# Stick-breaking attention by differences of neighbouring values

## The reference, cut to what matters

```python
z = einsum('bqhd,bshd->bhqs', qb, k) * HEAD_DIM ** -0.5
before = key_pos[None, :] < q_pos[:, None]
log_keep = where(before, log_sigmoid(-z), 0.0)
log_tail = cumsum(log_keep, axis=3, reverse=True) - log_keep
weight = where(before, exp(log_sigmoid(z) + log_tail), 0.0)
out = einsum('bhqs,bshd->bqhd', weight, v)
```

## Time and profile before

| | us |
|---|---|
| median of 3 runs (1811.06 to 1814.52) | 1811.9 |
| time of the profiled execution | 1813.25 |
| span of the profiled execution, first to last instruction | 1811.5 |
| TensorE busy in the span | 1668.0 (92%) |
| VectorE busy in the span | 1167.7 (64%) |
| projection of layer 1, first matmul with a weight to last copy | 1004.6 to 1148.2 |
| stick-breaking attention, first scores to last values | 1149.4 to 1236.8 |

### The profile page before, as it was taken

How to read it: one execution, slowest core, us unless ns; L and a number is a source line. 1 busy time by engine, 2 the same in 40 slices (tenths; PEclk the granted TensorE clock), 3 DMA queues, 4 the chain that set the end, 5 groups by cost and what they waited for, 6 DMA issues and landing times. The chain is left out here.

```text
span 1811.5 us, 27708 instructions
## 1 busy us (share of the span) xinstructions
PE 1668.0 (92%) x10992; PEld 893.3 (49%) x11121; DVE 1167.7 (64%) x1926; ACT 489.6 (27%) x854; POOL 180.2 (10%) x234
## 2 busy tenths in 40 slices
PE   6999988989979999999997999889989999999995
PEld 5656677855543333333332778654533333333332
DVE  5456877774347677767777533593337777777666
ACT  5243334453211111111112422573311111111112
POOL 2000734411000000000000000352100000000000
PEclk9999999989989999999998999999989999999997
DMA  6541000023779999999995220205679999999992
GB/s 166 157 126 36 7 3 3 4 94 116 306 300 418 425 426 428 424 427 425 427 425 213 94 93 24 93 2 220 270 315 425 426 426 426 426 426 426 426 422 113
DMA packets 101186, 471.45 MB, mean 260 GB/s; under 512 B 28864, under 2 KB 67776, under 8 KB 75456
## 3 DMA queue, kind: packets, MB, share of 16 engines
q1 hardware_dynamic: 98752, 461.25, 63.2%
q0 software_dynamic: 2304, 8.39, 1.2%
HBM read 452.84 MB, written 16.78 MB: 259 GB/s over the span
## 5 line engine op out<-in xcount | busy, mean ns | idle before, releaser
L707 PE MATMUL ps<-w_unit,xT 128*48 128x512 f32 x1024 | 454.6, 597 | 4.3 <-DVE xT L764 4.3
L708 PE MATMUL ps<-w_unit,xT 128*48 128x512 f32 x1024 | 454.7, 597 | 0.0
L809 DVE SCALAR_TENSOR_TENSOR x<-ps,gate_by_expert,x 128x512 f32<-128x512 f32 x512 | 348.4, 744 | 139.2 <-PE ps L759 139.0
L707 PEld LDWEIGHTS ps<-w_unit,xT 128*48 128x48 f32 x1024 | 126.6, 124 | 312.1 <-issue 306.6
L737 PE MATMUL ps<-w_unit,hidT 128*48 128x512 f32 x1024 | 249.3, 607 | 12.1 <-issue 12.1
L832 ACT ACTIVATE y_high_low<-y_cut 48x512 fp32r<-48x512 f32 x128 | 80.4, 628 | 403.8 <-DVE y_cut L780 401.4
L759 PE MATMUL ps<-y_high_low,slots_to_tokens 128*128 128x512 f32 x512 | 160.0, 434 | 13.8 <-DVE y_high_low L784 13.1
L759 PEld LDWEIGHTS ps<-y_high_low,slots_to_tokens 128*128 128x128 f32 x512 | 88.8, 194 | 133.2 <-issue 67.8
L1244 PE MATMUL ps<-hT_high,w_high 128*128 128x512 f32 (+1 forms) x344 | 140.0, 407 | 10.1 <-PE ps L1246 3.7
L1246 PE MATMUL ps<-hT_high,w_low 128*128 128x512 f32 (+1 forms) x344 | 136.2, 396 | 0.0
L1245 PE MATMUL ps<-hT_low,w_high 128*128 128x512 f32 (+1 forms) x344 | 135.8, 395 | 0.0
(11 more groups left out here) (365 smaller groups left out, 2241.9 us busy)
## 6 DMA issues: line engine op xcount, KB each, us to landing
w_unit<-in_moe_w SPq DMA_DIRECT2D x184, 2048.0 KB, 27.6
w_unit<-in_moe_w SPq DMA_DIRECT2D x16, 1024.0 KB, 32.3
x_rows<-sorted_rows SPq DMA_DIRECT2D x64, 192.0 KB, 26.2
w_unit<-in_od_w_qkv SPq DMA_DIRECT2D x12, 1024.0 KB, 5.4
w_raw<-in_ev_w_in SPq DMA_DIRECT2D x10, 1024.0 KB, 6.5
sorted_rows<-bias SPq DMA_DIRECT2D x32, 192.0 KB, 5.6
w_unit<-in_ev_w_out SPq DMA_DIRECT2D x2, 2048.0 KB, 11.9
w_unit<-in_od_w_out SPq DMA_DIRECT2D x2, 2048.0 KB, 10.4
```

Source lines behind the costliest of these rows:

```text
L707: nc.tensor.matmul(ps_1[0:MB, :], xT[b][:, k, :], w1[:, k, :], start=k == 0, stop=k == KD - 1)
L708: last = nc.tensor.matmul(ps_3[UP:UP + MB, :], xT[b][:, k, :], w3[:, k, :], start=k == 0, stop=k == KD - 1)
L809: nc.vector.scalar_tensor_tensor(out=xs, in0=ps_c[i % 4][:, :], scalar=gate(t), in1=xs, op0=ALU.mult, op1=ALU.add).then_inc(added, 1)
```

## The change

The sum over keys is taken by parts. Since beta = 1 - keep, the weight of key s is tail(s+1) - tail(s), and the output is the sum over s of tail(s) * (v(s-1) - v(s)), plus v of the last key. The kernel turns the tails themselves and multiplies them with the differences `dv`. In the last block of keys of a unit the last row is v(s-1) alone (`dv_last`), which puts the missing term back. beta, its mask and the product L1462 go; the tail tiles become four.

The differences are made in the projection. The column groups are permuted to v, q, k (`odd_columns`), so v is group 0 to 3. When all banks of v are emptied, SyncE copies v one key (one partition) down into `xn` by seven transfers inside SBUF: four of 127 partitions with 4 KB each and three of one row. They stand ahead of the weight load of group 7. GpSimd then waits for all seven, subtracts four tiles of 128x1024 and copies 127 rows of each difference back.

```diff
+def odd_columns(g):
+    lo = (g * GC + 2 * D) % (3 * D)
+    return slice(lo, lo + GC)
...
 class LoadedAhead:
-            sp.dma_start(self.raw[g], self.w[:, :, g * GC:(g + 1) * GC]).then_inc(self.raw_in[g], 16)
+            sp.dma_start(self.raw[g], self.w[:, :, odd_columns(g)]).then_inc(self.raw_in[g], 16)
...
 def odd_project(...):
-    is_v = lambda g: g >= 2 * D // GC
+    shifted, edge, differed, copied = c.sem("v_shifted"), c.sem("v_edge"), c.sem("v_differed"), c.sem("v_copied")
+    VG, QG = D // GC, 2 * D // GC
+    is_v = lambda g: g < VG
...
+    def shift(sp):
+        for t in range(TT):
+            sp.dma_start(xn[1:P, t, :], v[0:P - 1, t, :]).then_inc(shifted, 16)
+            if t:
+                sp.dma_start(xn[0:1, t, :], v[P - 1:P, t - 1, :]).then_inc(shifted, 16)
...
         @block.sync
         def _(sp):
             for g in range(w.RAW, NG):
-                w.load(sp, g, [(0, w_dram.rearrange("(p k) n -> p k n", k=KD)[:, :, g * GC:(g + 1) * GC])])
+                if g == VG + w.RAW:
+                    for b, (_, emptied) in enumerate(sems):
+                        sp.wait_ge(emptied, VG * TT // 8)
+                    shift(sp)
+                w.load(sp, g, [(0, w_dram.rearrange("(p k) n -> p k n", k=KD)[:, :, odd_columns(g)])])
+        @block.gpsimd
+        def _(pool):
+            pool.wait_ge(shifted, 16 * (2 * TT - 1))
+            nc.gpsimd.memset(xn[0:1, 0, :], 0.0).then_inc(edge, 1)
+            pool.wait_ge(edge, 1)
+            for t in range(TT):
+                nc.gpsimd.tensor_tensor(v[:, t, :], xn[:, t, :], v[:, t, :], ALU.subtract).then_inc(differed, 1)
+                pool.wait_ge(differed, t + 1)
+                nc.gpsimd.tensor_copy(xn[0:P - 1, t, :], v[0:P - 1, t, :]).then_inc(copied, 1)
+            pool.wait_ge(copied, TT)
...
 def stick_breaking(...):
-    beta = [c.sb(f"beta{i}", [P, 2, T], ctx=ctx) for i in range(DEEP)]
-    tail = [c.sb(f"tail{i}", [P, 2, T + 1], ctx=ctx) for i in range(2)]
+    tail = [c.sb(f"tail{i}", [P, 2, T], ctx=ctx) for i in range(DEEP)]
...
-                    pe.wait_ge(beta_done, 2 * (u - 2) + 2)
+                    pe.wait_ge(keep_done, u - 1)
...
-                pe.wait_ge(weighted, u + 1)
+                pe.wait_ge(scanned, 2 * u + 2)
...
-                                                   beta[u % DEEP][:, a, b * P:(b + 1) * P], c.ident[:, :])
+                                                   tail[u % DEEP][:, a, b * P:(b + 1) * P], c.ident[:, :])
...
-                                                v[:, b, h * HD:(h + 1) * HD], wT[u % 2][:, a, b * P:(b + 1) * P],
+                                                (dv_last if b == t else dv)[:, b, h * HD:(h + 1) * HD], wT[u % 2][:, a, b * P:(b + 1) * P],
...
-                    nc.scalar.activation(beta[i % DEEP][:, :, 0:L], ps_z[i % 2][:, :, 0:L],
-                                         ACT.Sigmoid).then_inc(beta_done, 1)
...
-                nc.vector.tensor_tensor(beta[i % DEEP][:, :, 0:L], beta[i % DEEP][:, :, 0:L],
-                                        tail[i % 2][:, :, T - L + 1:T + 1], ALU.mult).then_inc(weighted, 1)
```

More of the change, by code:

```diff
@@ L1264, in dest @@
         if is_v(g):
-            lo = g * GC - 2 * D
-            return v[:, s, lo:lo + GC]
-        f = FG * g + s
+            return v[:, s, g * GC:(g + 1) * GC]
+        f = FG * (g - VG) + s
         return qT[:, f, :] if f < KD else kT[:, f - KD, :]
@@ L1279, in empty_and_split @@
                 b = banks[n % 8]
-                b.empty(copy(dest(g, s), b.read(eng)[:, 0:width(g)], HD ** -0.5 if g < D // GC else 1.0))
+                b.empty(copy(dest(g, s), b.read(eng)[:, 0:width(g)], HD ** -0.5 if VG <= g < QG else 1.0))
             if n + 1 < len(outs) and outs[n + 1][0] != g and g + 2 < NG:
@@ L1327, in stick_breaking @@
 @stage
-def stick_breaking(nc, c, ctx, ps, qT, kT, v, yT, w_out, wts):
+def stick_breaking(nc, c, ctx, ps, qT, kT, dv, dv_last, yT, w_out, wts):
     PAIRS = C_HEADS // 2
@@ L1334, in stick_breaking @@
     keep = [c.sb(f"keep{i}", [P, 2, T], ctx=ctx) for i in range(DEEP)]
-    beta = [c.sb(f"beta{i}", [P, 2, T], ctx=ctx) for i in range(DEEP)]
-    tail = [c.sb(f"tail{i}", [P, 2, T + 1], ctx=ctx) for i in range(2)]
+    tail = [c.sb(f"tail{i}", [P, 2, T], ctx=ctx) for i in range(DEEP)]
     wT = [c.sb(f"wT{i}", [P, 2, T], ctx=ctx) for i in range(2)]
     zero = c.sb("zero", [P, T], ctx=ctx)
-    z_done, beta_done = c.sem("z_done"), c.sem("beta_done")
-    keep_masked, beta_masked = c.sem("keep_masked"), c.sem("beta_masked")
-    scanned, weighted = c.sem("scanned"), c.sem("weighted")
+    z_done, keep_done, keep_masked, scanned = c.sem("z_done"), c.sem("keep_done"), c.sem("keep_masked"), c.sem("scanned")
     turned, wT_out, pv_done, y_out, ready = (c.sem("turned"), c.sem("wT_out"), c.sem("pv_done"),
@@ L1417, in _ @@
                         act.wait_ge(scanned, 2 * (i - DEEP + 1))
-                        act.wait_ge(turned, i - DEEP + 1)
                     nc.scalar.activation(keep[i % DEEP][:, :, 0:L], ps_z[i % 2][:, :, 0:L], ACT.Sigmoid,
-                                         scale=-1.0).then_inc(beta_done, 1)
-                    nc.scalar.activation(beta[i % DEEP][:, :, 0:L], ps_z[i % 2][:, :, 0:L],
-                                         ACT.Sigmoid).then_inc(beta_done, 1)
+                                         scale=-1.0).then_inc(keep_done, 1)
                 u = i - LAG_T
@@ L1437, in _ @@
                 lo, hi = t * P, (t + 1) * P
[L1439 to L1443, removed]
+                pool.wait_ge(keep_done, i + 1)
+                part = keep[i % DEEP][:, :, lo:hi]
+                nc.gpsimd.affine_select(out=part, in_=part, compare_op=ALU.is_gt, fill=1.0, base=0,
+                                        pattern=[[0, 2], [-1, P]], channel_multiplier=1).then_inc(keep_masked, 1)
         @block.vector
@@ L1447, in _ @@
             nc.vector.memset(zero[:, :], 0.0).then_inc(ready, 1)
-            for i in range(2):
-                nc.vector.memset(tail[i][:, :, T:T + 1], 1.0).then_inc(ready, 1)
-            dve.wait_ge(ready, 3)
+            dve.wait_ge(ready, 1)
             for i, (t, f) in enumerate(units):
@@ L1453, in _ @@
                 dve.wait_ge(keep_masked, i + 1)
-                if i >= 2:
-                    dve.wait_ge(weighted, i - 1)
+                if i >= DEEP:
+                    dve.wait_ge(turned, i - DEEP + 1)
                 for a in range(2):
-                    nc.vector.tensor_tensor_scan(tail[i % 2][:, a, T - L:T][:, ::-1],
+                    nc.vector.tensor_tensor_scan(tail[i % DEEP][:, a, 0:L][:, ::-1],
                                                  keep[i % DEEP][:, a, 0:L][:, ::-1], zero[:, 0:L], 1.0,
                                                  ALU.mult, ALU.add).then_inc(scanned, 1)
-                dve.wait_ge(beta_masked, i + 1)
-                dve.wait_ge(scanned, 2 * i + 2)
-                nc.vector.tensor_tensor(beta[i % DEEP][:, :, 0:L], beta[i % DEEP][:, :, 0:L],
-                                        tail[i % 2][:, :, T - L + 1:T + 1], ALU.mult).then_inc(weighted, 1)
 def odd_mixer(nc, c, ps, x, gain, w_qkv, w_out, wts, slots, guests, ahead, held):
@@ L1472, in odd_mixer @@
         v = c.sb("v", [P, TT, D], ctx=inner)
+        xn = c.sb("xn", [P, TT, D], ctx=inner)
         with ExitStack() as proj:
-            xn = c.sb("xn", [P, TT, D], ctx=proj)
             odd_project(nc, c, proj, ps, x, xn, gain, w_qkv, qT, kT, v, ahead)
@@ L1477, in odd_mixer @@
         wts.add_units(guests, GUEST)
-        stick_breaking(nc, c, inner, ps, qT, kT, v, yT, w_out, wts)
+        stick_breaking(nc, c, inner, ps, qT, kT, v, xn, yT, w_out, wts)
     wts.add_units(slots, range(GUEST[0]))
```

## The result

The changed kernel takes 1860.47 us (median of 4 runs, 1857.82 to 1861.76), beside it the kernel before 1811.48 us; the ratio is 1.0275, 95% interval 1.0258 to 1.0291. It is slower by 49 us. Forecast were 1855 us and one transfer engine as the cause.

A forecast was written before the change was run, and what follows sets the result against it. VectorE was taken to bound the attention and TensorE the projection. The terms +2.4 + 0.3 + 52.5 + 2.5 - 14.5 = +43.2 us on the median 1811.9 gave 1855 us, range 1838 to 1902.

The forecast's parts named there:

- attention: Attention stage: without VectorE's product TensorE sets the pace, so the last filler starts earlier, -14.5 us.
- v first: Projection start: narrower v groups do less work while slices of x arrive, +2.4 us.
- last copy wider: Projection end: the last copy is twice as wide, +0.3 us.
- load 7 late: Projection: load 7 waits in SyncE's queue behind the one-engine shift, so group 7 starts late, +52.5 us.
- cold start after it: Projection, group 7: after idling, TensorE runs some 5 us at half speed, +2.5 us.
- GpSimd at the end: Projection end: GpSimd's eight instructions, at most 30 us, finish before the stage ends, 0 us.
- The deciding step: Shift in the projection: 127 rows go on one DMA engine (four tiles 79.1 us), not 16 (about 7 us).
- The speed of one engine: Shift: one DMA engine moves 26.3 GB/s, so a tile of 127 rows takes 19.8 us.
- D: Attention rival: it stays at its old pace because masks and hand-overs are late; 1870 us, chance 0.03.
- Rival A: Projection: the shift is spread over the engines and no load is late; -11.8 us, 1800 us, chance 0.12.
- B: Projection rival: one engine, but load 7 does not queue behind the shift; 1804 to 1818 us, chance 0.04.
- C: Shift rival: one engine at half the rate, +79 us on the forecast, 1934 us, chance 0.02.

The follow-up runs named there:

- experiments 5: Changed kernel without the shift and without GpSimd's differences, v still projected first: 1799.16 us, ratio 0.9942 to the kernel before.
- 9: Changed kernel with each 127-row transfer cut into 112 + 15 rows, run again as a base: 1799.65 us, ratio 0.9944 to the kernel before.
- experiments 1 to 3: Changed kernel with each 127-row transfer cut into 112 + 15, 122 + 5 and 111 + 16 rows, in this order: 1801.28, 1820.21 and 1808.58 us.
- Experiment 6: Changed kernel with loads 7 and 8 issued before the shift, its tiles one each behind loads 8 to 11: 1824.36 us, ratio 1.0077 to before.
- Experiment 8: Changed kernel with the same seven shift transfers issued from GpSimd's queue instead of SyncE's: 1801.84 us, ratio 0.9948 to the kernel before.
- experiment 3: Changed kernel with each 127-row transfer cut into 111 + 16 rows: 1808.58 us, ratio 0.9993 to the kernel before.

## Why the prediction was right, point by point

| term | forecast | measured | from |
|---|---|---|---|
| attention | -14.5 | -14.53 | 84.47 to 69.94 |
| v first | +2.4 | +4.07 | experiments 5, 9 against before |
| last copy wider | +0.3 | +0.2 | 0.60 us against 0.38 |
| load 7 late | +52.5 | +59.2 | the one wait of TensorE |
| cold start after it | +2.5 | +1.1 | 207.56 - 147.28 - 59.19 |
| GpSimd at the end | 0 | 0 | its last copy ends at 1163.9, the stage at 1209.9 |
| sum | +43.2 | +50.0 | medians: +49.0 |

The profiled executions differ by 48.2 us: beside these +50.0 the changed one was 2.9 us shorter ahead of the projection and 1.0 longer behind the attention, in stages that the change does not touch.

**The deciding step.** One engine for 127 rows was chosen between two far ends; no row of the kernel before could decide between them, and experiments 1 to 3 show it. That load 7 waits for the shift as the next in SyncE's order is shown by 6 (same rows and engine behind the loads, and 3.2 us of stall are left) and by the windows around 1130, where load 7 lacks the one engine. Experiment 8 takes the stall away too, but it also spreads the rows, so it does not tell the two apart. In detail SyncE was held as well: it issued load 7 only at 1126, for which I had no row.

**The speed of one engine.** 26.3 GB/s from the earlier trace rows against 26.1 from the line through experiments 1 to 3. The shift was longer than 79.1 us because of a part that does not depend on the engine: 6.5 us, of which I had counted about 1.

**The mis-sized term.** Load 7 late is +6.7 off. The shift took 86.1 us from its first issue where I had 80.1 (+6.0), but began 1.1 us earlier, and load 7 landed 2.4 us behind it and not 3.7 (-1.3). The split and its hand-over took 5.1 us instead of 3.5 (+1.6), beside GpSimd, where I allowed "under 1 us". TensorE had finished group 6 at 1090.7 and not at 1092.1, so it stood idle for 1.4 us more. The cold start was too dear: the granted clock was back after 3.0 us (1149.9 to about 1152.9) and not after 5.

**v first.** The mechanism (fewer columns while the slices arrive) was right for 2.4 us; the fall of the clock that it brings, 1.7 us, was missing. That this and the cold start (-1.4) nearly cancel is luck.

**The attention.** All four block lengths ran at TensorE's pace, and the straight line between 512 and 128 keys held (2.46 and 1.81 us from turn to turn where 2.45 and 1.81 were forecast). The argument against D was too strong: the earlier trace rows are an undisturbed cycle, and most of the short units before took about 1.39 us, with waits for VectorE, so that they gained as well.

**The rivals.** Rival A's time (1800) is what experiments 1, 9 and 8 measured (1801.3, 1799.7, 1801.8), and its limit of 27 us for a shift without a stall fits: 11.5 us gave none, and 31.5 us gave 4.6. The 36 us to break even lie between 31.5 (even in the medians; by its stages experiment 3 is still 4.4 us faster) and 45.0 (slower by 0.6%). B, C and D did not happen in the changed kernel. Experiment 6 is close to B's case and came out above B's 1804 to 1818, at 1824.4: there the tiles alternate with loads, and GpSimd ended at 1172.8 and not by 1169.

## What to carry to other kernels

A transfer's price is not in its bytes alone: ask how many engines it can be shared by, and row counts without a large divisor up to 16 are where to look: 127 went to one engine, 122 to two and 111 to three. A shift by one partition makes one of 127. Then ask what stands behind it on its queue and when that is due, because the price is paid there and not at the transfer. And when an edit removes work from the engine that was the bound, what it gives is the distance to the next engine, not the work removed: here 0.6 us in a unit of 512 keys, from which 1.23 us of VectorE's work went, and 0.2 us in one of 128.

## What the runs showed of the hardware that was not expected

- SyncE's issue of one transfer took up to 20.0 us when those before it sat on one engine, against 0.58 for a load in the kernel before.
- The granted clock can fall while a stage runs: in the changed kernel TensorE was busy for 0.42 us of the microsecond from 1002 to 1003, and the clock went to 0.50. The next microsecond shows 0.90 busy at 0.50, so a high busy share does not say that the clock is up.
- VectorE and GpSimd slow each other: a cut of 128x2048 took 2.00 to 2.79 us beside GpSimd and 1.22 alone, a split 3.00 and 2.29; GpSimd's subtraction of 128x1024 took 4.40 and, with VectorE idle (experiment 6), 2.34.
